# Backward streams and word-interleaved stationary operands in a split-precision decoder trunk

## The reference

```python
for layer in range(2):
    h = rms_norm(x, attn_norm[layer])
    proj = h @ w_in[layer]                  # 1024 x 7428: all mixers' inputs, forget and gate logits
    o = pool(..), diff_attention(..), stick_breaking(..), forgetting_attention(..)
    merged = sum(sigmoid(g_n + b_n) * (o_n @ w_branch[layer][rows_n]) for n in range(4))
    x = x + merged @ w_out[layer]           # 1024 x 1024
    h = rms_norm(x, ffn_norm[layer])
    gate, up = split(h @ w_ffn_up[layer])   # 1024 x 5632
    x = x + (silu(gate) * up) @ w_ffn_down[layer]   # 2816 x 1024
```

## Time and profile before

| | |
|---|---|
| median of 3 runs | 861.93 us (861.75 to 862.0) |
| profiled execution, span from its first to its last instruction | 859.8 us |
| TensorE matmuls in the profile | 4246, busy 855.7 us |
| weight loads of TensorE | 4246, busy 711.6 us |
| DVE / ACT / POOL busy | 593.9 / 446.0 / 113.6 us |
| granted TensorE clock, mean | 1.000 |
| DMA | 160.53 MB, 187 GB/s, 58.8% of the 16 engines' span on the main queue |

### The profile page before, as it was taken

The page is one execution under the profiler, slowest core; times in us unless marked ns, Lnnn a source line. Parts: engine busy times, 40 slices in busy tenths (PEclk is TensorE's granted clock), DMA queues, the critical chain, the costliest instruction groups (busy, mean ns, idle before and its releaser), DMA issues.

```text
span 859.8 us, 11140 instructions
## 1 busy us (share of the span) xinstructions
PE 855.7 (100%) x4246; PEld 711.6 (83%) x4246; DVE 593.9 (69%) x850; ACT 446.0 (52%) x646; POOL 113.6 (13%) x89
## 2 busy tenths in 40 slices
PE   9999999999999999999999999999999999999998
PEld 7888888888888888888888888888888888888887
DVE  7896967768777665564479768768696765565543
ACT  7567654854454444443364674558443644444431
POOL 0750101005401000000005401010063000000000
PEclk9999999999999999999999999999999999999999
DMA  9846656475657666555566465665665576665641
GB/s 343 290 150 190 200 175 183 148 228 180 188 184 236 190 195 190 182 185 189 162 186 178 119 195 158 196 197 162 205 196 179 151 234 183 185 190 177 195 147 50
DMA packets 87815, 160.53 MB, mean 187 GB/s; under 512 B 7505, under 2 KB 14161, under 8 KB 87761
## 3 DMA queue, kind: packets, MB, share of 16 engines
q1 hardware_dynamic: 87328, 159.16, 58.8%
q10 hardware_dynamic: 432, 0.66, 0.2%
HBM read 158.74 MB, written 1.05 MB: 186 GB/s over the span
## 4 chain that ended last, share of the span: by engine, by line
PE 93%; DVE 3%; DMA 2%; ACT 1%; SPq 1%; issue 0%; ACTq 0%
PE bulk L1692 28%; PE bulk L1696 28%; PE bulk L1693 28%; DMA raw<-in_w_in_dram 2%; DVE w_lo L1013 2%; PE bankAB L1432 1%; PE bankAB L1634 1%; PE bankT L1587 0%; PE bankAB L1576 0%; ACT w_hi L737 0%; PE bankAB L1441 0%; PE bankAB L1532 0%; PE bankO L1545 0%; PE bankT L1634 0%; PE bankO L1634 0%
## 5 line engine op out<-in xcount | busy, mean ns | idle before, releaser
L1013 DVE TENSOR_TENSOR w_lo<-raw,w_hi 128x1024 fp32r<-128x1024 f32 (+1 forms) x288 | 362.3, 1272 | 156.5 <-ACT w_hi L737 152.9
L737 ACT ACTIVATE w_hi<-raw 128x1024 fp32r<-128x1024 f32 (+1 forms) x286 | 297.7, 1049 | 245.3 <-PE bulk L1696 240.8
L1692 PE MATMUL bulk<-w_hi,hT_hi 128*128 128x512 f32 (+1 forms) x880 | 344.1, 391 | 0.2 <-DVE w_lo L1013 0.2
L1693 PE MATMUL bulk<-w_lo,hT_hi 128*128 128x512 f32 (+1 forms) x880 | 339.2, 385 | 0.0
L1696 PE MATMUL bulk<-w_hi,hT_lo 128*128 128x512 f32 (+1 forms) x880 | 336.5, 386 | 0.0
L1692 PEld LDWEIGHTS bulk<-w_hi,hT_hi 128*128 128x128 f32 x880 | 165.3, 188 | 33.2 <-DVE w_lo L1013 0.7
L1696 PEld LDWEIGHTS bulk<-w_hi,hT_lo 128*128 128x128 f32 x880 | 165.0, 188 | 33.4
L1693 PEld LDWEIGHTS bulk<-w_lo,hT_hi 128*128 128x128 f32 x880 | 165.4, 188 | 31.7
L1692 PE MATMUL bulk<-w_hi,aT_hi 128*128 128x512 f32 x174 | 68.0, 391 | 0.0
L1696 PE MATMUL bulk<-w_hi,aT_lo 128*128 128x512 f32 x174 | 67.7, 389 | 0.0
L1693 PE MATMUL bulk<-w_lo,aT_hi 128*128 128x512 f32 x174 | 67.7, 389 | 0.0
(11 more groups left out here) (259 smaller groups left out, 720.7 us busy)
## 6 DMA issues: line engine op xcount, KB each, us to landing
raw<-in_w_in_dram SPq DMA_DIRECT2D x110, 512.0 KB, 4.1
raw<-in_w_ffn_up_dram SPq DMA_DIRECT2D x80, 512.0 KB, 4.4
raw<-in_w_ffn_down_dram SPq DMA_DIRECT2D x44, 512.0 KB, 3.3
raw<-in_w_branch_dram SPq DMA_DIRECT2D x20, 512.0 KB, 4.2
raw<-in_w_out_dram SPq DMA_DIRECT2D x16, 512.0 KB, 3.4
bias<-in_b_gate_dram SPq DMA_DIRECT2D x16, 256.0 KB, 4.4
raw<-in_w_ffn_up_dram SPq DMA_DIRECT2D x16, 256.0 KB, 3.2
raw<-in_w_in_dram SPq DMA_DIRECT2D x10, 256.0 KB, 2.7
```

The costliest lines, as they stand in the source:

```text
L737: act.activation(w_hi[:, g % RING, :, 0:width], raw[:, g % RAW, :, 0:width], ACT.Copy).then_inc(hi_ready, 1)
L1013: vec.tensor_tensor(w_lo[:, g % RING, :, 0:width], raw[:, g % RAW, :, 0:width], w_hi[:, g % RING, :, 0:width].bitcast(F32), ALU.subtract). ...
L1692: pe.matmul(dst, hi, whi, start=(k == ks[0]), stop=False)
L1693: pe.matmul(dst, hi, wlo, start=False, stop=False)
```

## The change

Three things, in one diff.

- `interleaved` puts the hi and the lo part of `hT`, `oT` and `aT` in one buffer, word by word: hi, lo, hi, lo. A stationary operand is now 128 words at a distance of 8 bytes, so it reaches over 1024 bytes. The buffer starts 32 words (128 bytes) past a multiple of `PERIOD` = 256 bytes.
- `backward` issues a wide product with the streamed operand and the PSUM destination both reversed: the last column is read first and written first. The result is the same. It replaces the plain product in `multiply`, `first_unit` and for the last columns.
- `queries` is aligned to 256 bytes in place of 2048. (The stages' small products keep their form.)

```diff
+PERIOD = 256
+SHIFT = 32
...
+        def interleaved(name, blocks, stack):
+            whole = sb(name, [P, SHIFT + blocks * SEQ * 2], F32R, stack, PERIOD)[:, SHIFT:]
+            both = whole.rearrange("p (k q two) -> p two k q", k=blocks, two=2)
+            return [both[:, part, :, :] for part in range(2)]
...
-        hT = [sb("hT_hi", [P, KD, SEQ], F32R, align=LINE), sb("hT_lo", [P, KD, SEQ], F32R, align=LINE)]
+        hT = interleaved("hT", KD, ctx)
...
-        oT = [sb("oT_hi", [P, 10, SEQ], F32R, mixing, LINE), sb("oT_lo", [P, 10, SEQ], F32R, mixing, LINE)]
+        oT = interleaved("oT", 10, mixing)
-        queries = [sb(f"queries_{part}", [P, 4, SEQ], F32R, mixing, LINE) for part in ("hi", "lo")]
+        queries = [sb(f"queries_{part}", [P, 4, SEQ], F32R, mixing, PERIOD) for part in ("hi", "lo")]
...
-        aT = [sb("aT_hi", [P, KF, SEQ], F32R, ffn_area, LINE), sb("aT_lo", [P, KF, SEQ], F32R, ffn_area, LINE)]
+        aT = interleaved("aT", KF, ffn_area)
...
+            def backward(dst, stationary, streamed, start, stop):
+                return pe.matmul(dst[:, ::-1], stationary, streamed[:, ::-1], start=start, stop=stop)
...
-                            pe.matmul(dst, hi, whi, start=(k == ks[0]), stop=False)
-                            pe.matmul(dst, hi, wlo, start=False, stop=False)
+                            backward(dst, hi, whi, start=(k == ks[0]), stop=False)
+                            backward(dst, hi, wlo, start=False, stop=False)
...
-                            ins = pe.matmul(dst, lo, whi, start=False, stop=(k == ks[-1] or g == DEPTH * U - 2 and i == 1 and t == 1))
+                            ins = backward(dst, lo, whi, start=False, stop=(k == ks[-1] or g == DEPTH * U - 2 and i == 1 and t == 1))
```

More of the change, by code:

```diff
@@ L1719, in high @@
                     for t in range(TT):
-                        pe.matmul(item_bank(0, 0, t), hT[0][:, k, t * P:(t + 1) * P], w_hi[:, u, k % 2, :], start=(k == 0), stop=False)
+                        backward(item_bank(0, 0, t), hT[0][:, k, t * P:(t + 1) * P], w_hi[:, u, k % 2, :], start=(k == 0), stop=False)
                 def low(k):
@@ L1725, in low @@
                     for t in range(TT):
-                        pe.matmul(item_bank(0, 0, t), hT[1][:, k, t * P:(t + 1) * P], w_hi[:, u, k % 2, :], start=False, stop=False)
+                        backward(item_bank(0, 0, t), hT[1][:, k, t * P:(t + 1) * P], w_hi[:, u, k % 2, :], start=False, stop=False)
                 for k in tiles:
@@ L1738, in first_unit @@
                     for k in tiles:
-                        ins = pe.matmul(item_bank(0, 0, t), hT[0][:, k, t * P:(t + 1) * P], w_lo[:, u, k % 2, :], start=False,
-                                        stop=k == KD - 1)
+                        ins = backward(item_bank(0, 0, t), hT[0][:, k, t * P:(t + 1) * P], w_lo[:, u, k % 2, :], start=False,
+                                       stop=k == KD - 1)
                     if last and t == 0:
@@ L1789, in _ @@
                     whi, wlo = w_hi[:, last % RING, i, columns], w_lo[:, last % RING, i, columns]
-                    pe.matmul(dst, hi, whi, start=(i == 0), stop=False)
-                    pe.matmul(dst, hi, wlo, start=False, stop=False)
-                    ins = pe.matmul(dst, lo, whi, start=False, stop=(i == 1))
+                    backward(dst, hi, whi, start=(i == 0), stop=False)
+                    backward(dst, hi, wlo, start=False, stop=False)
+                    ins = backward(dst, lo, whi, start=False, stop=(i == 1))
                 ins.then_inc(last_columns_done, 1)
```

## The result

The changed kernel takes 881.48 us (median of 3 runs, 881.39 to 881.54) against 861.93 us: 1.0228 of the time before, with an interval of 1.0208 to 1.0248. It is slower by 19.6 us, where 827 us had been predicted; the time lies outside the range of 820 to 856. Its profiled execution has a span of 879.7 us (before 859.8) at a granted clock of 1.00, with as many matmuls and loads as before.

A forecast was written before the change was run, and what follows sets the result against it. TensorE's wide products were taken as the bound: 859.8 - 33.6 (wide) - 1.0 (narrower) - 2.2 (transients) + 1.5 (waits) = 824.5 us profiled; the median 2.1 us above gives 826.6, predicted 827, range 820 to 856.

The forecast's parts named there:

- What bounds the kernel: TensorE's chain: the three wide products of `multiply` hold 84% of it, so each nanosecond between their starts counts.
- What the 11 ns are: Per fp32r product on TensorE, some 11 ns lost to collisions of the stream and load readers, depending on addresses and phase.
- Part one: Wide products: interleaved operands and falling streams keep both readers half a 256-byte period apart, cutting 226.7 ns to 216.
- the wide products: The 3138 wide products behind the start were to save 10.7 ns each, 33.6 us.
- the narrow ones: The 108 narrower products, of 260 or 256 columns, were to save 9 ns each, 1.0 us.
- the 1.5 us for waits: Time added for TensorE waiting where DVE's work is denser than its mean; ends 0 and 6 us.
- The 216 ns: Forecast distance of 512-column wide products: columns plus the bf16 warm-up's 2.4 to 2.7 ns, no collisions left.
- the mild form of the backward stream: Rival, each wide product: falling addresses handled worse, at the transient's 236 ns, 891 us; chance 0.10.
- The start: Before 59.8 us DMA and DVE set the pace, so 216 faster products there gain 0; at most 2.3 us.
- What is late next: With units of twelve falling from 2.72 to 2.59 us, DVE rises from 77% to 81% busy; 1.5 us of waits.
- the operands' writes: ACT and DVE storing every second word of the stationary operands was to cost 0, at most 5 us.
- The last columns: At the end, nine products of 256 columns were to take 0.98 us in place of 1.08.

The follow-up runs named there:

- e10: Kernel before, but 512-column wide products read the stream and write PSUM in 16-byte lines, every fourth line, in four passes: 857.85 us, ratio 0.996.
- e12: e10 with each stationary buffer 56 words past a multiple of 256 bytes: 850.63 us, 0.9871 of the kernel before.
- e6: Kernel before with each stationary buffer 32 words (128 bytes) past a multiple of 256 bytes: 879.48 us.
- e8: Kernel before with each stationary buffer 64 words past a multiple of 256 bytes: 861.71 us, ratio 0.9999.
- m1: No decoder: 31 groups of 48 products alone, varying direction, step and stationary start; 226.7 ns in the form of before, 233.3 in that of the change.
- m3: No decoder: 37 groups of 48 products in other stream orders and stationary starts; 2 to 8 falling blocks, rising inside, 226.7 to 227.1 ns.
- e3: The changed kernel with SHIFT = 0 in place of 32, so stationary operands start at a multiple of 256 bytes: 884.34 us.
- m4: No decoder: 34 groups of 48 products varying the number of stationary columns and the stream's order of 16-byte lines; every fourth line 223.5 ns.
- e5: Kernel before with wide products reading the stream rising but writing PSUM falling, output columns mirrored: 861.81 us.
- e9: The changed kernel with rising stream and write, still interleaved, and SHIFT = 16 in place of 32: 873.83 us.
- e11: e10 with runs of 8 words in place of lines of 4, every fourth run: 863.53 us, 1.0026 of the kernel before.
- m2: No decoder: 44 groups of 48 products varying stationary and stream starts, widths and heights; rising, stationary start at 128 words 226.7 ns, at 24 words 234.4.
- m5: No decoder: 39 groups of 48 products around the every-fourth-line order; stream and PSUM both in it 223.5 ns, PSUM alone 227.1.

## Why the prediction was wrong

**What bounds the kernel** was right. TensorE's chain of wide products set the time before and sets it after, and the change of the distance times their number gives the whole difference (19.8 by the mean distances, 19.9 measured). A nanosecond on the distance costs some 3.3 us, and held in both directions: the mean distances of `e10` and `e12` give 3.9 and 11.0 us, and 3.7 and 11.1 were measured.

**What the 11 ns are** is the step that failed, and "Part one" with it. The prediction took the loss above 216 ns for collisions between the stream and the load, which a constant phase half a period apart would remove. Three parts of that have to be told apart.

- That the loss is a matter of two readers: mostly wrong. With one stationary column the rising stream has 231.5 to 231.9 ns, and with one word streamed again and again it has 218.7 with the full load beside it. Most of the loss is the stream's own. The load in step takes 5 ns off it (226.7), out of step it adds up to 3 (234.4). How the load does that is open.
- That phase counts, with a period of 256 bytes: right. `e6` (+17.7 us for 128 bytes) and `e8` (nothing for 256 bytes) show it in the decoder. But of the places tried with 128 rising columns none is better than the same start, half a period away has 232.3, and the kernel before was already there, since everything was aligned to 2048 bytes. Nor does the 8-byte step help a rising stream: its ten starts have 230.0 to 234.0 ns (`m1`, `m3`). The transient of the earlier trace rows was read as proof that 226.7 was bad luck of the phase; what it settled at was the good case.
- That falling addresses at the load's speed would free the product of collisions: they do fix the distance (no transient, and 233.3 ns at every start tried in the small kernel; 234.2 with `hT` in `e3`), but at the high end: a read that falls inside 256 bytes leaves no good phase. In the sum the wide products were to give -33.6 us and gave +22.1, the narrow ones were to give -1.0 and gave next to nothing, and the 1.5 us for waits were not needed: 55.7 + 1.0 - 1.5 = 55.2 us, of a miss of 54.5.

The 216 ns took a floor from bf16 products, columns plus 2.4 ns. None of the groups with 512 fp32r columns has less than 218.5 ns, not even with one stationary word and one streamed word (`m4`, L83: 302.36 - 291.87 us over 48). So 2.5 ns of the 10.7 that were to be won are in no phase.

**The rival that held** is the mild form of the backward stream, at a chance of 0.10. Its price was taken from the worst distance in the trace, 236 ns and 891 us; 233.3 ns and 881.5 us were measured. Its other half, the write, is free (`e5`, `m1` L62). The trace of before had no falling address, and this should have weighed more: the gain rested on a model in which a direction that no row showed had only advantages.

**The start** was to be pinned by the first weights, which the trace of `e12` bears out for faster products: there TensorE comes on the chain at 59.78 us, as at 59.79 before. Slower ones are not hidden there: TensorE itself is on the chain from 0.97 us on (the chain in order of time, above), and in the first 59.8 us it gets 298 instructions done where the earlier trace rows have 303. The same columns as there, for the kernel after:

```profile
0.00:59.80 59.80, 58.83 (x298) 49.47 (x298) 49.02 (x86) 35.91 (x54) 22.94 (x28) 1.00 0.75 272
```

**What is late next, and the operands' writes.** TensorE did not wait for DVE by more than 0.8 us in all, but since it got no faster this tests nothing. In `e12`, at 223.8 ns, all waits of TensorE and its loads for a `w_lo` are 2.3 us; 216 ns were never reached. Writing word by word was costed at nothing; it is nothing for DVE and 57 ns for ACT on a store of 512 columns; ACT's total grew by 1.7 us, with 432 us free there. Right in time, wrong in "nothing in the rows makes their distance count".

**The last columns** were to go from 1.08 to 0.98 us; they went to 1.06. Right in sign, and for 256 columns only.

**What stays open.** So the failed step is known, but the cause of 226.7 and 233.3 ns is not. Open are: why a load that ends with a 256-byte period makes the product shorter; why a stream that walks through more than one 16-byte line costs 8 to 25 ns more than one that stays in a line; why every fourth line, with starts of 0 or 56 words, is better; and why one form of product has two distances in one kernel (`e3`, `e9`, `e11`, `e12`). The two orders were found by search. The runs show what they give, not why.

## What to carry to other kernels

A loss per product that changes with phase is not yet a collision that can be removed: before a layout is changed for it, measure the exact pair of patterns in groups of 48 products, and include the null cases, one stationary column and one streamed word. Then measure the kernel itself: the groups had the sign right for `e9`, `e10` and `e12` but two to three times the size, and for `e11` not even the sign. In a kernel like this one keep fp32r streams rising inside each 256 bytes, and let a stationary operand of 128 columns and the streamed one start at the same place of a 256-byte period; 128 bytes ahead of a buffer cost this kernel 2%. Where a change uses a direction or a step that the trace does not show, the chance of a loss there should be near that of the gain.

## What the runs showed of the hardware

- The distance of fp32r products of 512 columns at the 2.4 GHz level (granted clock 1.00) goes by addresses alone from 218.7 (one 16-byte line) over 275 (lines of 4 words, every 16th; `m4`, L73: 191.72 - 178.50 us over 48) to 451 (every second word) and 461 ns (every fourth word; `m3`, L75). In bf16 the direction costs nothing. The timelines of `m1` and `m2`, each for a long stretch; a shorter one with the same start holds six products in 1.46 us in both:

```profile
326.74 9.44 PE L87 MATMUL banks<-Wb,Sb 128*128 128x512 bf16 x43
```

```profile
465.29 8.58 PE L102 MATMUL banks<-Wb,Sb 128*128 128x512 bf16 x39
```

  Rising, 37 more products take 7.98 us, 215.7 ns each; falling, 33 take 7.12 us, 215.8 ns.
- The stationary operand's start alone moves the distance from 226.7 to 234.4 ns, with everything else the same; with 96 to 127 columns it is the end that goes with the good distance (`m4`). The rule of the Trainium skill ("TensorE: Matmul & The Clock Gate", "What happens when you issue a matmul") that the two read ports are independent does not agree with that (by it the start would not matter), though it comes nearer than the prediction did: most of the loss is there without a load.
- The rule on PSUM that the prediction cited ("Advanced Engine Details and Errata", "PSUM Cachelines", in the Trainium skill) does not agree, as far as any non-contiguous pattern is said to slow a product: in `e5` a reversed write cost 0.06 us in 861.8, and a write of four words at every fourth place had 227.1 ns (`m5`, L62). Whether single words apart cost something no run here shows.
- A load is longer at a step of 8 bytes (193 ns in the change), and by more at 12 and 16 bytes (253 and 309 ns in `m2` and `m3`), and yet the distance there, shorter than the load, was only 237 and 235 ns.
